# A level-by-level block inversion on TensorE: where a step's dense pieces stand among its two sums

## The reference, cut to what matters

```python
def wkv7_scan(r, w, k, v, a_vec, b_vec):              # 8 heads of 64, 512 tokens
    def step(state, inp):
        r_t, w_t, k_t, v_t, a_t, b_t = inp
        sa = jnp.einsum('bhvk,bhk->bhv', state, a_t)
        state = (state * w_t[:, :, None, :] + sa[..., None] * b_t[:, :, None, :]
                 + v_t[..., None] * k_t[:, :, None, :])
        return state, jnp.einsum('bhvk,bhk->bhv', state, r_t)
...
def memory_cross_attention(h, mem_n, w_q, w_kv, w_o):
    k, v = jnp.split(mem_n @ w_kv, 2, axis=-1)        # 256 x 1024 @ 1024 x 2048
...
```

## Time and profile before

| what | us |
|---|---|
| median of 3 runs | 1666.3 (1666.15 to 1667.53) |
| the profiled execution, its own time | 1669.42 |
| span of the profiled execution | 1667.3 |
| TensorE busy | 1611.6 (97%) |
| VectorE busy | 883.6 (53%) |
| ScalarE busy | 659.9 (40%) |
| GpSimd busy | 113.3 (7%) |
| the inversion's loop, from `y_sum(0)` to the last dense piece | about 81 |

### The profile page before, as it was taken

One profiled execution on the slowest core, in us unless ns is written; L12 is line 12 of the kernel. 1 busy time (PEld: TensorE's weight loads), 2 busy tenths in 40 slices (PEclk: granted clock), 3 DMA queues, 4 the chain that ended last, 5 costly groups with the idle time before them and its releaser, 6 DMA issues.

```text
span 1667.3 us, 26139 instructions
## 1 busy us (share of the span) xinstructions
PE 1611.6 (97%) x11311; PEld 1285.5 (77%) x11311; DVE 883.6 (53%) x1330; ACT 659.9 (40%) x958; POOL 113.3 (7%) x141
## 2 busy tenths in 40 slices
PE   7989999999999999999999989999899999999998
PEld 5856769877776678888888868777558788888887
DVE  6454586441544355545444654435975755555644
ACT  4315743323444255424241244456884422221220
POOL 2200105100000000000000020012300000000000
PEclk9999999999999999999999999999999999999999
DMA  7711222321451244645444542222003233333222
GB/s 232 185 53 51 76 87 92 104 75 45 135 182 38 91 151 127 216 127 192 148 159 158 170 116 83 57 74 73 1 14 111 66 89 101 101 102 101 88 83 83
DMA packets 153460, 176.59 MB, mean 106 GB/s; under 512 B 14504, under 2 KB 111410, under 8 KB 152962
## 3 DMA queue, kind: packets, MB, share of 16 engines
q1 hardware_dynamic: 142424, 156.82, 29.7%
q10 hardware_dynamic: 10922, 18.11, 3.6%
HBM read 168.31 MB, written 8.43 MB: 106 GB/s over the span
## 4 chain that ended last, share of the span: by engine, by line
PE 79%; DVE 6%; PEld 5%; ACT 4%; issue 2%; DMA 2%; POOL 1%; ACTq 1%; SPq 0%; PEldq 0%; POOLq 0%; DVEq 0%
PE ps L392 65%; PEld ps L392 2%; PEld ps L1315 2%; PE ps L1551 2%; PE ps L1315 1%; DMA sb_arena<-sb_arena 1%; DVE weights_low L415 1%; PE ps L2827 1%; PE ps L1773 1%; PE ps L2584 1%; PEld ps L1321 1%; PE ps L899 1%; PE ps L2572 1%; PE ps L2604 1%; DVE sb_hT L2680 1%
## 5 line engine op out<-in xcount | busy, mean ns | idle before, releaser
L392 PE MATMUL ps<-left_high,weights_high 128*128 128x512 f32 (+1 forms) x1016 | 404.4, 398 | 8.1 <-DVE left_low L698 3.1
L415 DVE TENSOR_TENSOR weights_low<-sb_weights_raw,weights_high 128x2048 fp32r<-128x2048 f32 (+1 forms) x118 | 266.3, 2256 | 259.6 <-ACT weights_high L412 259.5
L392 PE MATMUL ps<-left_low,weights_high 128*128 128x512 f32 (+1 forms) x1016 | 396.9, 391 | 0.0
L392 PE MATMUL ps<-left_high,weights_low 128*128 128x512 f32 (+1 forms) x1016 | 396.7, 390 | 0.0
L412 ACT CAST weights_high<-sb_weights_raw 128x2048 fp32r<-128x2048 f32 (+1 forms) x118 | 221.3, 1876 | 308.5 <-PE ps L392 261.2
L392 PEld LDWEIGHTS ps<-left_high,weights_high 128*128 128x128 f32 (+1 forms) x1016 | 190.7, 188 | 62.4 <-issue 13.2
L392 PEld LDWEIGHTS ps<-left_high,weights_low 128*128 128x128 f32 (+1 forms) x1016 | 190.9, 188 | 41.1
L392 PEld LDWEIGHTS ps<-left_low,weights_high 128*128 128x128 f32 (+1 forms) x1016 | 191.0, 188 | 40.7 <-issue 1.7
L392 PE MATMUL ps<-weights_high,hidden_high 128*128 128x512 f32 x432 | 169.0, 391 | 0.0
L392 PE MATMUL ps<-weights_high,hidden_low 128*128 128x512 f32 x432 | 168.2, 389 | 0.0
L392 PE MATMUL ps<-weights_low,hidden_high 128*128 128x512 f32 x432 | 168.1, 389 | 0.0
(11 more groups left out here) (419 smaller groups left out, 2125.0 us busy)
## 6 DMA issues: line engine op xcount, KB each, us to landing
sb_weights_raw<-in_w_in SPq DMA_DIRECT2D x25, 1024.0 KB, 5.2
sb_yT<-in_ada_w SPq DMA_DIRECT2D x24, 1024.0 KB, 5.2
sb_weights_raw<-in_ffn_w_up SPq DMA_DIRECT2D x44, 512.0 KB, 4.5
sb_weights_raw<-in_mlp_w_up SPq DMA_DIRECT2D x16, 1024.0 KB, 6.2
sb_weights_raw<-in_mlp_w_down SPq DMA_DIRECT2D x16, 1024.0 KB, 7.7
sb_weights_raw<-in_ffn_w_down SPq DMA_DIRECT2D x10, 1024.0 KB, 4.9
sb_weights_raw<-in_xattn_w_kv SPq DMA_DIRECT2D x8, 1024.0 KB, 5.4
sb_weights_raw<-in_w_out SPq DMA_DIRECT2D x6, 1024.0 KB, 4.9
```

What stands on the lines that cost most here:

```text
L392: last = nc.tensor.matmul(o, lhsT, rhs, start=b["first"] and i == 0, stop=b["last"] and i == len(pairs) - 1)
L415: nc.vector.tensor_tensor(l[:, 0:n], raw[:, 0:n], h[:, 0:n].bitcast(F32), ALU.subtract).then_inc(w_low, 1)
```

## The change

Only TensorE's program is changed, and in it only the order within a step: all but one of the step's dense pieces now stand ahead of `x_sum(i-1)`, and one behind it. The number of pieces of each step, their order among themselves, and every wait are the same. The programs of ScalarE, VectorE, GpSimd and SP are untouched.

```diff
             for i in range(N_INV + 1):
                 if i < N_INV:
                     y_sum(i)
+                fill(dense, INV_FILL[i] - 1)
                 if i:
                     x_sum(i - 1)
-                fill(dense, INV_FILL[i])
+                fill(dense, 1)
```

## The result

The changed kernel took 1675.94 us (median of 4 runs, 1674.9 to 1678.1) where the kernel before took 1666.22 us (4 runs, 1665.5 to 1667.53). The ratio is 1.005, with a 95% interval of 1.0038 to 1.0062, that is 6.3 to 10.3 us more. It is slower, as forecast; the forecast was 7.2 us more and 1673.5 us, in a range from 1670.8 to 1677.0.

A forecast was written before the change was run, and what follows sets the result against it. TensorE was taken as the bound, busy all 81.0 us of the inversion's loop. Extra groups cost 3.6 + 2.6 + 1.0 = 7.2 us, so 1666.3 + 7.2 = 1673.5 us, range 1670.8 to 1677.0.

The forecast's parts named there:

- one dense group as two: Steps 1 to 19 of the inversion's loop: each gets one more dense group at 0.19 us, 3.6 us in all.
- Both sums as two groups in levels 1 to 4: 16 steps of the loop: y and x sums apart cost 0.16 us more each, 2.6 us in all.
- Level 5: Steps 17 to 19: y and x sums apart lose their overlap, 0.33 us each, 1.0 us in all.
- the 0.23 us pause: Step 14 of the loop in the kernel before: no releaser in the profile, so the forecast left it in.
- The x sum alone: An x sum with no y sum directly ahead, levels 1 to 4: taken as 1.09 us, upper bound 1.25.
- The restart of step 14: The x sum of step 14 pauses and starts again from nothing; its records gave 1.07 to 1.08 us for a lone x sum.
- Rival B: A lone x sum starts slowly, its halves not side by side, and costs 1.25 us: 9.7 us more, 1676.0; chance 0.13.
- Nothing behind the loop takes it back: Everything behind the loop is a chain starting at the barrier, so the 7.2 us stay in the kernel's time.
- the barrier: End of the loop: with one piece behind the last x sum TensorE is still last by 0.16 us, so unchanged cost.
- Rival C: Half or more of the groups' cost is hidden, the 0.19 us belonging to semaphore waits: 1669.9 us; chance 0.08.
- Rival D: Half-clock stretches behind the inversion vanish, half of 20.5 us comes back, kernel faster at 1663.3 us; chance 0.03.
- The estimate by 166 ns: Alternative sum from the isolated product's latency: 38 changes of mode at 0.166 us, 6.3 us; not used in the forecast.

The follow-up runs named there:

- the probe: Kernel before plus unused TensorE products behind the inversion's loop, alternating tile shapes and number formats in five sections; 64x64 float32 against 128x128 float32r took 0.33 us there and back.
- the pairs kernels: Kernel before with steps joined two by two on TensorE, ScalarE and VectorE: 1671.85 us, ratio 1.0013; with most of the memory's weight transfers left out, 1665.3 us.
- five joined pairs: Kernel before with only steps 4 and 5, 6 and 7, 8 and 9, 12 and 13, 14 and 15 joined: 1669.67 us, ratio 1.001.

## Why the prediction was right

**The sum.** Its three terms, with what the changed kernel shows: one dense group as two, forecast 3.6 us, measured 3.8 (0.19 each in steps 1 to 10, 0.19 to 0.22 with 512 columns). Both sums as two groups in levels 1 to 4, forecast 1.08 + 1.09 - 2.01 = 0.16 each and 2.6 in all; measured 1.08 + 1.09 - 2.01, 2.5 in all. Level 5, forecast 1.0; measured 3 x 0.32. Together 7.3, and the loop is longer by 7.0, as it also lost the 0.23 us pause, which the prediction left in. That the pause went was no part of the forecast, and it brought the loop nearer to the forecast's 88.2 than the terms alone would.

**The x sum alone** was the one unknown price. The restart of step 14 gave 1.07 to 1.08 us, the prediction took 1.09, and 1.09 was measured. Rival B (1.25 us, 9.7 us in all) fell on the first step: the crossed and the uncrossed halves run side by side from the first record (264.60 and 264.62 above). That a pause in a trace shows what a start from rest takes was worth more than the nearest regular row.

**Nothing behind the loop takes it back**, and the barrier costs what it did: the same 0.50 us from the last dense start to the next stage's first product, with one piece as cover instead of two. The run with no piece behind the last x sum shows how near the edge that was, 0.84 us of waiting.

**Rival C** (half of the cost hidden) fell with the loop, and its reason with the probe: alternations without any semaphore between them cost 0.33 us there and back, where step 1 lost 0.35. **Rival D** (the clock) acted, as a disturbance: between these two profiles it gave back 1.1 us behind the loop (6.5 to 5.5), and the stretches differed between any two profiles of the same kernel. It never came near 10 us.

**The size.** The first median was 9.7 us up and 2.4 us above the forecast, still in the range. By itself it would have spoken for rival B, whose time was 1676.0; it is the loop, and not the time of the whole kernel, that decides between the two. The loop is 7.0 us in each of three profiles, the comparisons give about 8.3, 6.4 and 8.5 us. Whether there is a further microsecond in executions without a profile stays open; the records show none in fixed places.

**The rule on tiling.** The Trainium skill, "TensorEngine Tiling (Array Packing)", Key Properties, has a change of mode drain the array and a change of tile not. The runs agree as far as a price can show it: 0.28 to 0.37 us there and back between modes in the probe, while y and x sums on different quarters of the array overlap in the kernel. The estimate by 166 ns of the Trainium skill's "TensorE: Matmul & The Clock Gate", Single matmul latency, 6.3 us, came within 1 us of the 7.3 measured; that section is about one product alone and not about a change of mode, so the nearness may be chance.

**What the prediction did not have.** It left the pause of step 14 without a cause. It is a place where TensorE's next packet of instructions had landed only 1.57 us before. That this can stop TensorE was not in the prediction at all, and decided only the experiments that went the other way.

## What to carry to other kernels

Where small-tile and full-array products share TensorE, count the groups and not only the products: each further pair of changes costs 0.33 to 0.38 us here (0.5 where two sums of level 5 also lose their overlap), and it buys nothing while no consumer is late. Before putting work between two dependent pieces look for a wait that it would cover; the waits view of TensorE had none. And to join groups isn't free either: long bursts of small products outran the packets of instructions here, while the dense pieces between shorter groups left the packets time. A pause that stands in the middle of a sum, with "issue" as its releaser, is worth counting: see whether the records from one such pause to the next come to a whole number of packets.

## What the runs showed of the hardware

- A change of tile shape there and back, 64x64 or 64x128 against 128x128, costs 0.28 to 0.37 us; from float32 to float32r with the whole array, nothing that the rows show.
- Groups of 192 records of 64x64 products (3.73 us from first to last start) with full-array groups of 3.6 to 3.8 us between them paused by 0.4 to 3.5 us, 3 or 4 of 8 in the pairs kernels and 3 of 5 with five joined pairs, each pause ending 1.3 to 1.6 us after a 16 KB packet of the instruction queue had landed, and each at the same place in a count of 256 of TensorE's records. Groups of 96 records paused once in the profile of before, by 0.2 us and at such a place, and groups of 32 and 64 in the changed kernel never.
- A 1 MB weight load can hold such a packet back, in these runs one in the loop: with the load it started 4.4 to 4.5 us after the group's first record and the longest pause was 3.5 us, without it 1.6 and 0.8.
